# A two-block transformer kernel: the second model's layers start with the first pair's gate tiles

## The reference, cut to what matters

```
mod = silu(c) @ w_ada[l] + b_ada[l];  shift, scale, gate = split(mod, 3)
h = rms_norm(x, norm_g[l]) * (1 + scale) + shift
gq, gk, gv, glr, gz, dq, dk, dv, dz = split_columns(h @ w_in[l])
gq, gk, gv = split(silu(causal_depthwise_conv(concat(gq, gk, gv), conv_w[l])))
log_a = log_sigmoid(glr @ w_gk + b_gk) / 16            # cumulated per chunk of 64 tokens
o_gla  = rms_norm(gated linear attention(gq, gk, gv, log_a), g_out) * silu(gz)
o_diff = rms_norm(differential attention(dq, dk, dv)) * silu(dz)
x = x + gate * (concat(o_gla, o_diff) @ w_out[l])
```

## Time and profile before

| | |
|---|---|
| median of 3 runs | 1962.71 us |
| the profiled execution's own time | 1966.36 us |
| its span, first to last instruction | 1964.6 us |
| TensorE matmuls busy | 1852.8 us (94%) |
| VectorE, ScalarE, GpSimd busy | 1060.0, 877.7, 875.4 us |
| mean granted TensorE clock | 0.978 of full speed |

### The profile page before, as it was taken

The page is one execution under the profiler, slowest core; times in us unless marked ns, Lnnn a source line. Parts: engine busy times, 40 slices in busy tenths (PEclk is TensorE's granted clock), DMA queues, the critical chain, the costliest instruction groups (busy, mean ns, idle before and its releaser), DMA issues.

```text
span 1964.6 us, 26448 instructions
## 1 busy us (share of the span) xinstructions
PE 1852.8 (94%) x8566; PEld 1448.0 (74%) x8566; DVE 1060.0 (54%) x1731; ACT 877.7 (45%) x1385; POOL 875.4 (45%) x1064
## 2 busy tenths in 40 slices
PE   7999989999999999999899999998999988999988
PEld 5666667887888788888788778886776656776756
DVE  5666646612643577787566115523665553674561
ACT  6667643411433455655444214323554533554441
POOL 3323246655665334344147556653543315443323
PEclk9999999999999999999899999998999988999999
DMA  4111125433543222112145334422222112222212
GB/s 151 59 60 53 54 59 167 161 96 107 166 134 96 86 65 65 63 54 66 43 150 171 96 107 153 155 88 75 86 65 65 54 43 86 72 69 65 65 43 75
DMA packets 49660, 176.36 MB, mean 90 GB/s; under 512 B 5649, under 2 KB 5777, under 8 KB 49569
## 3 DMA queue, kind: packets, MB, share of 16 engines
q1 hardware_dynamic: 42368, 148.99, 24.5%
q10 hardware_dynamic: 7200, 26.22, 4.0%
HBM read 173.08 MB, written 2.10 MB: 89 GB/s over the span
## 4 chain that ended last, share of the span: by engine, by line
PE 76%; DVE 10%; ACT 7%; issue 5%; POOL 1%; DMA 0%; DVEq 0%; ACTq 0%; SPq 0%; POOLq 0%
PE ps_g L234 22%; PE ps_g L238 21%; PE ps_g L241 21%; PE ps_zt L939 2%; PE ps_s L1429 1%; PE ps_o L1490 1%; PE ps_o L967 1%; ACT w_hi L206 1%; PE ps_o L495 1%; DVE scr L1603 1%; PE ps_zt L485 1%; PE ps_s L386 1%; DVE scr L1125 1%; PE ps_zt L477 1%; DVE scr L443 1%
## 5 line engine op out<-in xcount | busy, mean ns | idle before, releaser
L214 POOL TENSOR_TENSOR w_lo<-raw,w_hi 128x256 fp32r<-128x256 f32 x936 | 764.6, 847 | 899.5 <-ACT w_hi L206 899.0
L206 ACT ACTIVATE w_hi<-raw 128x1024 fp32r<-128x1024 f32 x274 | 288.9, 1054 | 383.3 <-PE ps_g L241 378.0
L234 PE MATMUL ps_g<-h_hi,w_hi 128*128 128x512 f32 x1424 | 407.0, 414 | 32.7 <-ACT h_hi L295 11.6
L238 PE MATMUL ps_g<-h_lo,w_hi 128*128 128x512 f32 x1424 | 377.7, 394 | 0.9 <-DVE h_lo L267 0.9
L241 PE MATMUL ps_g<-h_hi,w_lo 128*128 128x512 f32 x1424 | 374.9, 392 | 0.3 <-DVE w_lo L222 0.3
L234 PEld LDWEIGHTS ps_g<-h_hi,w_hi 128*128 128x128 f32 x1424 | 259.5, 191 | 119.0 <-issue 54.2
L238 PEld LDWEIGHTS ps_g<-h_lo,w_hi 128*128 128x128 f32 x1424 | 270.6, 190 | 61.6 <-DVE h_lo L267 2.0
L241 PEld LDWEIGHTS ps_g<-h_hi,w_lo 128*128 128x128 f32 x1424 | 270.0, 190 | 58.4 <-DVE w_lo L222 0.7
L234 PE MATMUL ps_g<-a_hi,w_hi 128*128 128x512 f32 x768 | 206.5, 405 | 16.8 <-DVE a_lo L1637 7.5
L238 PE MATMUL ps_g<-a_lo,w_hi 128*128 128x512 f32 x768 | 197.8, 393 | 0.0
L241 PE MATMUL ps_g<-a_hi,w_lo 128*128 128x512 f32 x768 | 197.6, 393 | 0.0
(11 more groups left out here) (167 smaller groups left out, 2027.1 us busy)
## 6 DMA issues: line engine op xcount, KB each, us to landing
raw<-weights SPq DMA_DIRECT2D x274, 512.0 KB, 3.5
scr<-ada_weights ACTq DMA_DIRECT2D x48, 512.0 KB, 4.1
x<-x_tiles SPq DMA_DIRECT2D x8, 256.0 KB, 5.7
y<-x SPq DMA_DIRECT2D x8, 256.0 KB, 3.3
scr<-csil_dram ACTq DMA_DIRECT2D x2, 512.0 KB, 4.9
lvmask<-level_masks SPq DMA_DIRECT2D x1, 512.0 KB, 8.4
mats<-squares SPq DMA_DIRECT2D x1, 448.0 KB, 6.8
vecs<-vectors SPq DMA_DIRECT2D x1, 95.5 KB, 2.0
```

The source lines that it names most:

```text
L206: nc.scalar.activation(w_hi[:, t.rep % 2], raw[:, raw_slot(t)], ACT.Copy).then_inc(whi_ready, 1)
L214: ins = nc.gpsimd.tensor_tensor(w_lo[:, t.rep % 2, ks], raw[:, raw_slot(t), ks], w_hi[:, t.rep % 2, ks].bitcast(F32), ALU.subtract)
L234: nc.tensor.matmul(bank[:], w_hi[:, t.rep % 2, kk], rhs(k)[0], start=(first and n == 0), stop=False)
L238: nc.tensor.matmul(bank[:], w_hi[:, t.rep % 2, kk], rhs(k)[1], start=False, stop=False)
```

## The change

1. The two z tiles of the first GLA pair come first (tiles 0 and 1), then glr (tile 2), then the pair's four convolution tiles (3 to 6); the other tiles keep their places.
2. Tiles 0 and 1 work on x times gain (norms "4" and "6", made with `early_hi` and `early_lo` while the tiles ahead finish, so 8 activations and 8 VectorE operations more per layer). VectorE multiplies their results by the root into `z_b`. What the shift adds, W's, is made by 8 float32 matmuls of one column for each of the two tiles (`shift_pe`), copied by ScalarE.
3. The full h is made as before, into the other pair of buffers (`h_buf` swaps `h_hi`, `h_lo` with `a_hi0`, `a_lo0`), with a copy of tile 0 and tile 1 out of PSUM and two `split_hi` among its steps. Tiles 2 and 3 take it in halves, in turn.
4. The silu of tiles 0 and 1 is spread over later halves: `zlog` (four activations: absolute value, add W's, exp, ln), `zmin`, `zexp`, the product.
5. The decay gate moves from the pair's halves 0 and 1 to its halves 3 and 5, after that half's taps. It has its own buffer.
6. The absolute value of the convolution tiles moves from VectorE to ScalarE, into the `ln` step.

In the diff, the parts are the lists, TensorE's start, ScalarE's start, `zlog` and `ln` on ScalarE, and VectorE's start.

```diff
+        OWN["gla0"] = {i: list(OWN["gla"][i]) for i in OWN["gla"]}
+        for _i, _z in ((5, 0), (9, 1)):
+            OWN["gla0"].setdefault(_i, []).append(("zlog", _z))
+            OWN["gla0"].setdefault(_i + 2, []).append(("zmin", _z))
+            OWN["gla0"].setdefault(_i + 4, []).extend([("zexp", _z), ("evac3", 4 + _z)])
...
                     if it[0] == "gla":
-                        due[0].append(("gate", it[1]))
-                        due[1].insert(0, ("gate2", it[1]))
+                        due[3].append(("gate", it[1]))
+                        due[5].append(("gate2", it[1]))
...
+        def start_pe(pe, l):
+            T, n = T_B2 + l * B2_TILES, 5 + 2 * l
+            first = b2_rhs(n - 1)
+            shift_pe(pe, l, 0)
+            gemm(pe, At(T), T, first, H1, True, False, h_waits(n - 1), (x_ready, (6 + l) * KT - 1))
+            norm_pe(pe, 4 + l)
+            gemm(pe, At(T), T, first, H2, False, True, h_waits(n - 1))
+            shift_pe(pe, l, 1)
+            gemm(pe, At(T + 1), T + 1, first, ALL, True, True, None, (x_ready, (6 + l) * KT))
+            hi, lo = h_buf(n)
+            for half in (H1, H2):
+                for i in (2, 3):
+                    t, slot, bank = At(T + i), (T + i) % 2, ps_g[(T + i) % 2]
+                    pe.wait_ge(whi_ready, t.of(1, 1))
+                    pe.wait_ge(*reader(i - 2, l))
+                    for k, _ in half:
+                        pe.wait_ge(hhi_ready, KT * n + k + 1)
+                        nc.tensor.matmul(bank[:], w_hi[:, slot, k], hi[:, k], start=(k == 0), stop=False)
+                    for k, _ in half:
+                        pe.wait_ge(h_ready, KT * n + k + 1)
+                        nc.tensor.matmul(bank[:], w_hi[:, slot, k], lo[:, k], start=False, stop=False)
+                    if half is H2:
+                        pe.wait_ge(wlo_ready, t.of(1, 1))
+                        for k in range(KT):
+                            ins = nc.tensor.matmul(bank[:], w_lo[:, slot, k], hi[:, k], start=False, stop=(k == KT - 1))
+                        ins.then_inc(tile_used, 1)
...
+                if s[0] == "start":
+                    rstd_act(act, 4 + l)
+                    for k in range(KT):
+                        norm_hi(act, l, k)
+                        if k == 1:
+                            split_hi(act, At(T + R_TILE))
+                        elif k == 3:
+                            act.wait_ge(ws_done, 2 * l + 2)
+                            act.activation(ws_b, ps_o[:, 0:2], ACT.Copy).then_inc(ws_ready, 2)
+                        elif k == 5:
+                            split_hi(act, At(T + R_TILE + 1))
+                    split_hi(act, At(T + R_TILE + 2))
...
+                elif s[0] == "zlog":
+                    act.activation(g_ls.buf, u, ACT.Abs, bias=ws).then_inc(g_ls.abs_ready, 1)
+                    act.wait_ge(g_ls.abs_ready, n.v + 1)
+                    act.activation(u, u, ACT.Identity, bias=ws)
+                    g_ls.act(act, n)
...
+                elif s[0] == "ln" and it[0] == "gla" and s[1] < 4:
+                    act.wait_ge(cv_done, (l * GLA_PAIRS + it[1]) * 12 + 3 * c + 3)
+                    act.wait_ge(b_ls.ready, n.v)
+                    act.activation(b_ls.buf, cv_b[c % 2], ACT.Abs).then_inc(b_ls.abs_ready, 1)
+                    b_ls.act(act, n)
...
+                if s[0] == "start":
+                    for k in range(KT):
+                        if k == 2:
+                            nc.vector.memset(acc[:], 0.0).then_inc(acc_zero, 1)
+                        if k >= 2:
+                            norm_lo(dve, l, k - 2)
+                        norm_tmp(dve, l, k)
+                        if k in (3, 6):
+                            i = k // 4
+                            dve.wait_ge(tile_used, T + i + 1)
+                            nc.vector.tensor_tensor(z_b[i], ps_g[(T + i) % 2][:], rstd_x, ALU.mult).then_inc(z_out, 1)
```

More of the change, by code:

```diff
@@ L1294, in schedule @@
         def schedule():
-            steps = [("gemm", 0, 0), ("gemm", 0, 1), ("gate_in",)]
+            steps = [("start",), ("gate_in",)]
             left = {}
@@ L1298, in schedule @@
             for it in ITEMS + [None]:
[L1299 to L1300 removed]
+                first = it == ITEMS[0]
+                n = 0 if it is None else (8 if first else 12 if it[0] == "gla" else 8)
+                due = [list(left.get(i, [])) for i in range(20)]
                 if it:
[L1302 to L1303 removed]
+                    own = OWN["gla0" if first else it[0]]
+                    for i in own:
+                        due[i] += [s + (it,) for s in own[i]]
                     if it[0] == "gla":
[L1305 to L1306 removed]
+                        due[3].append(("gate", it[1]))
+                        due[5].append(("gate2", it[1]))
                 if before:
@@ L1311, in schedule @@
                 for half in range(n):
-                    steps.append(("gemm", FIRST_TILE[it] + half // 2, half % 2))
+                    if not first or half >= 2:
+                        steps.append(("gemm", FIRST_TILE[it] + half // 2, half % 2))
                     steps += due[half]
-                left = {i - n: due[i] for i in range(n, 16) if due[i]}
+                left = {i - n: due[i] for i in range(n, 20) if due[i]}
                 if it is None:
                     steps.append(("split",))
-                    for i in range(16):
+                    for i in range(20):
                         steps += due[i]
@@ L1327, in build_program @@
         SWISH = [s[1:] for s in STEPS if s[0] == "evac3"]
-        SILUS = [s if s[0] == "gate" else s[1:] for s in STEPS if s[0] == "gate" or s[1:] in SWISH and s[0] == "evac"]
+        SILUS = [s[1:] for s in STEPS if s[1:] in SWISH and s[0] == "evac"]
         def nth(order, key, l):
@@ L1353, in build_program, with log_of @@
         b_ls, b_turn = LogSig("b_ls", bls_b), Turn("b_turn", ps_t)
+        g_ls, LOGS = LogSig("g_ls", res[1][4]), [s for s in STEPS if s[0] in ("gate", "zlog")]
+        z_b, ws_b = [scr2[:, 14], scr2[:, 15]], sml[:, 61:63]
+        ws_done, ws_ready, z_out = ev("ws_done"), ev("ws_ready"), ev("z_out")
+        def log_of(s, l):
+            g_ls.buf = res[1][4] if s[0] == "gate" else scr2[:, 12 + s[1]]
+            return nth(LOGS, s, l)
         b_unit = Unit("b_unit", M_HEADS, DH, bsq_b, brstd_b)
@@ L1407, in b2_pe @@
                 it = s[-1]
-                if s[0] == "gemm":
+                if s[0] == "start":
+                    start_pe(pe, l)
+                elif s[0] == "gemm":
                     tile, half = s[1], s[2]
-                    gemm(pe, At(T + tile), T + tile, h_rhs, H2 if half else H1, not half, bool(half),
-                         h_waits(4 + l) if tile == 0 else None,
-                         reader(tile - 2, l) if tile >= 2 and not half else None)
+                    gemm(pe, At(T + tile), T + tile, b2_rhs(5 + 2 * l), H2 if half else H1, not half, bool(half), None,
+                         None if half else reader(tile - 2, l))
                 elif s[0] == "gate":
@@ L1698, in b2_pool @@
             for s in STEPS:
-                if s[0] == "gemm" and s[2] == 0:
+                if s[0] == "start":
+                    for i in range(2):
+                        pool.wait_ge(ws_done, 2 * l + i + 1)
+                        split_lo(pool, At(T + i + 1))
+                    split_lo(pool, At(T + R_TILE + 1))
+                    split_lo(pool, At(T + R_TILE + 2))
+                elif s[0] == "gemm" and s[2] == 0:
                     split_lo(pool, At(T + s[1] + 1))
@@ L1716, in build_program @@
                 for name in ("ng00", "ng01", "ng10", "ng11")]
+        GAIN += [lambda d, l=l: mod[:, l, bass.ds(d + KT, 1)] if not isinstance(d, int) else mod[:, l, KT + d:KT + d + 1]
+                 for l in range(2)]
         @block.sync
```

154 lines of the change are left out of this document (89 added, 65 removed).

## The result

Slower. The changed kernel takes 1972.12 us (median of 9 runs, 1968.9 to 1977.58); beside it on the same chip the kernel before took 1963.08 (1962.11 to 1965.26, 9 runs): ratio 1.0046, 95% interval 1.0035 to 1.0057, so 9.0 us more. I had forecast 1957.2 (1946 to 1967), faster. The profiled execution of the changed kernel took 1977.38, its span is 1975.4; that is 10.8 over the span before. The nine runs fall into two groups, 1968.9 to 1969.74 at a mean clock of 0.983 or 0.984 and 1975.12 to 1977.58 at 0.979 to 0.982, with the median between them; the profiled execution is one of the upper group.

A forecast was written before the change was run, and what follows sets the result against it. TensorE's matmuls (94% of the span) were taken to bind, then the convolution loop (5.82 a turn for a 5.44 tile). The starts' 11.3 and 11.2 shrink to 2.75 per layer: 2 x 2.75 = 5.5, 1962.7 - 5.5 = 1957.2; range 1946 to 1967.

The forecast's parts named there:

- A: Moment when the start's first four tiles are done and the next begins; forecast 1379.1 and 1684.2, 11.3 and 11.2 earlier.
- three signs of being wrong: Tile 4 not starting before 1385; six turns under 41 or over 48; low clock in over two short stretches, 1410 to 1445.
- the six turns: ScalarE's taps-to-taps times from the second to the eighth taps: 8.7, 6.3, 9.8, 4.9, 9.75, 6.2, sum 45.7.
- 13.2: Length of VectorE's norm chain in the start: 11.75 before, plus the memset (0.3) and two PSUM copies of 0.65 each.
- taps 2 to 3 ... 6.3: First pair's turn in the GLA loop: zlog's four activations (2.96) lie beside VectorE's taps, so 6.3.
- taps 2 to 3: 6.2: Second pair's turn from taps 2 to taps 3 in the GLA loop, the last of six, claimed at 6.2.
- two longer turns: Turns from taps 1 to 2 in both pairs, with the gate ahead of the split: 8.7 and 9.75.
- Those pauses cost nothing more while the clock holds.: TensorE's waits in the GLA stretch, some 1.6 for tile 9 and 3 for tile 10, claimed to add nothing further.
- third rival: Clock falls in new pauses ahead of tile 10; TensorE loses 8.2, the kernel is 7 slower, 1969.8; chance 0.13.
- first rival: VectorE slowed by its neighbour: z's four operations take 1.22 instead of 0.69, 1 to 2 on the chain, 1960.7; chance 0.27.
- second rival: Convolution loop doesn't bind, so the start's 11.2 stay in both layers: 1940.2, chance 0.10; half of it, 1948, 0.08.
- From there to the layer's end nothing is changed.: From the layer's first statistic to its end, no change in time; a shift stays a shift.

The follow-up runs named there:

- x4: Changed kernel with only the first of four pieces of each second-model w_lo made, the rest left out; 1953.29 us, ratio 0.9945 to the kernel before.
- x2: Changed kernel with both pairs' gate2 (minimum and scans) one half later, at half 6; 1972.32 us, ratio 1.0041 to the kernel before.
- x8: Kernel before with only the gate's steps moved to halves 3 and 5, with its own buffer for the logarithm; 1977.99 us, ratio 1.0069.
- x1: Changed kernel with the second pair's gate back at its first two halves; 1966.5 us, ratio 1.0010 to the kernel before.
- x14: x10 with both gates' matmul ahead of the second tile and their activations between the first two taps; 1956.51 us, ratio 0.9961 to the kernel before.
- x15: x14 with the convolution tiles' absolute value back on VectorE; 1955.87 us, ratio 0.9956 to the kernel before.
- x5: Kernel before with only the first of four pieces of each second-model w_lo made, the control for x4; 1957.72 us, ratio 0.9963.
- x13: Kernel before with each convolution tile's exp and logarithm behind the next tile's taps on ScalarE; 1970.81 us, ratio 1.0030.
- x10: x6 with the first pair's gate between its first and second taps, its absolute value on ScalarE; 1959.77 us, ratio 0.9970 to the kernel before.
- x12: x10 with both gates between the first two taps, and each tile's absolute value, exp and logarithm behind the next tile's taps; 1966.14 us, ratio 1.0004.
- x3: Changed kernel with the convolution tiles' absolute value back on VectorE; 1975.89 us, ratio 1.0063 to the kernel before.
- x6: x1 with z's activations cut apart and put ahead of each even half's exp; 1963.29 us, ratio 0.9996 to the kernel before.
- x9: Kernel before with only the convolution tiles' absolute value moved from VectorE to ScalarE; 1972.55 us, ratio 1.0044.

## Why the prediction was wrong

By the marks of the first table, the profiled span is some 16 longer than forecast (10.8 longer than before, not 5.5 shorter). Of this, 5.6 lies in the two starts (2.2 in each from the norm's sum to A, 1.2 ahead of the two sums), 8.0 between A and the statistic, nearly all of it in the turns, and 2.6 behind the second statistic. Of the three signs of being wrong that I had named, one came: the six turns add up to over 48.

**The new start: right in kind, 2 us short.** The first pair's work on x without the root keeps TensorE busy and at 2.4 GHz (1.00 in both windows). The sum came at 1357.36 (1356.9 forecast); the shift matmuls took 1.84 for 16 (1.70 until the next matmul started), where I took 1.0 within bounds of 0 to 2.0. In the second layer, where the first of them stands ahead of the sum, this is the 0.7 by which it is later than forecast. VectorE's first product came 2.51 after the sum, for 2.66; of the 1.0 more before, which I put down to the fallen clock, 0.4 was the memset that stood ahead of the product (1359.21). A came 24.4 after the sum, not 22.2. The term "13.2" of VectorE's norm chain was mis-sized: it ran 16.0 (from 1359.87 to 1375.9). Its timeline shows operations of 1.1 and more for 0.75, and beside them `w_lo`'s four pieces 4.29 for 2.82. ScalarE waits for these operations, so its second split ended 11.2 after the chain's start, not 9.9, and TensorE, for which I had no wait there, stood 1.31 for it.

```profile
1363.85 1.11 DVE L307 SCALAR_TENSOR_TENSOR scr<-x,mod,scr 128x512 f32<-128x512 f32 x1
1364.89 0.68 DVE L1689 TENSOR_TENSOR scr<-ps_g,scr 128x512 f32<-128x512 f32 x1
1365.49 1.32 DVE L302 SCALAR_TENSOR_TENSOR a_lo<-scr,mod,a_hi 128x512 fp32r<-128x512 f32 x1
...
1369.32 0.75 DVE L302 SCALAR_TENSOR_TENSOR a_lo<-scr,mod,a_hi 128x512 fp32r<-128x512 f32 x1
```
```profile
1357.02 2.82 POOL L215 TENSOR_TENSOR w_lo<-raw,w_hi 128x256 fp32r<-128x256 f32 x4 [5.49 <-ACT w_hi L207]
1363.12 4.29 POOL L215 TENSOR_TENSOR w_lo<-raw,w_hi 128x256 fp32r<-128x256 f32 x4 [3.28 <-ACT w_hi L207]
```

x4 takes three of four pieces away, the chain runs 14.0 and A comes after 22.49: those 1.9 are shown to be the split's. Before, the chain ran with no split beside it (the last piece ended at 1358.90, the chain began at 1359.61), and I had put two there without a price. The Trainium skill, "GPSIMD Engine Reference", Specifications, says that VectorE's instructions with two SBUF inputs collide with GpSimd on their shared interface; the rows agree (the copy at 1364.89, which reads PSUM, took its 0.68).

**The failing step: "taps 2 to 3 ... 6.3", and "taps 2 to 3: 6.2".** They took 8.64 and 7.79, which is 3.9 of the 4.1 by which the six turns exceed my 45.7; the others were close (8.52, 10.63, 4.91, 9.32 for 8.7, 9.8, 4.9, 9.75). The step failed twice. I followed ScalarE's queue and asked of VectorE only when the minimum comes: I left out that the taps themselves wait for the silu product of two tiles earlier, and that gate2 puts nine instructions ahead of it on VectorE. And with those nine in the sum, at the 1.57 that the scans take in the earlier trace rows, the turn would still have come out near 6.5: beside the split the scans took 3.71. The taps' wait for the product is 2.10, and the scans are 2.14 longer. Neither half does it alone. With gate2 moved away (x2) the first pair's turn is 6.45. With most of the split cut but gate2 in place (x4) the two turns are 7.09 and 6.52. So the order puts VectorE's queue into ScalarE's turn, and in the first pair nearly all of the wait is VectorE slowed beside GpSimd's split.

**The gate's place.** I priced its two longer turns and still let the start's gain cover them. With the split as it is, it doesn't: the place alone costs 13.5 in the old order (x8), and in the changed kernel one gate put back gives 7 (x1). With both gates where ScalarE idles and z's activations in its gaps the kernel is 7.7 (x14) and 8.6 (x15) faster than before by the ratios. Of the 20.5 by which the changed kernel's two starts are shorter, x14 has 12.4 left at its two statistics.

**"Those pauses cost nothing more while the clock holds."** It did not hold. TensorE stands 2.87 ahead of tile 9, whose bank the late taps 0 set free (the row at 1418.37; forecast 1.6), and 0.63 for `w_hi` ahead of tile 10 (forecast 3). The windows at tile 9 show the low level, 1.2 GHz. The last two rows are the second layer's, one at the same pause of 2.87 and one ahead of the statistic:

```profile
1416.40:1418.30 1.90, 0.00 (x0) 0.00 (x0) 1.83 (x4) 0.98 (x3) 1.41 (x3) 0.96 0.00 0
1418.40:1420.00 1.60, 1.60 (x4) 1.31 (x5) 1.60 (x3) 1.54 (x3) 1.60 (x2) 0.50 0.00 0
1420.00:1423.20 3.20, 3.20 (x14) 2.55 (x14) 3.13 (x5) 1.36 (x3) 0.59 (x1) 0.76 0.33 106
1423.20:1428.00 4.80, 4.17 (x19) 3.09 (x19) 1.97 (x5) 3.54 (x6) 1.29 (x2) 1.00 0.11 42
...
1725.20:1732.20 7.00, 5.37 (x13) 4.14 (x14) 6.89 (x10) 3.64 (x7) 3.69 (x4) 0.51 0.25 70
1756.00:1759.60 3.60, 3.60 (x12) 2.82 (x11) 2.09 (x3) 2.09 (x4) 0.16 (x1) 0.53 0.43 148
```

So the third rival's mechanism came, one tile earlier than it said. In the first layer it was far cheaper than its 8.2: 1.6 at the low level and about half of the next 3.2, so 3.1 us in which TensorE lost 1.6. In the second layer it was dearer. The clock's shortfall in the last two rows (0.49 of 7.00 and 0.47 of 3.60) is 5.1, some of it while TensorE was waiting anyway, and the way from A to the statistic is 1.4 longer there than in the first layer. The rival's time (1969.8) was near, but the clock is the smaller part of the way to it.

The first rival, VectorE slowed by its neighbour, was right in kind and closer to the cause than my forecast was. It named the four operations of z and priced them at 1 to 2; the dear ones were the scans (3.71 for 1.57) and the start's. The second rival, that the loop doesn't bind, fell (x5, x13).

**"From there to the layer's end nothing is changed."** It takes 2.2 and 2.6 longer. The first of these is the next start: there the norm's sum stands behind the shift matmuls and half a gemm, and comes 6.4 after the last eight out matmuls begin (1659.58 to 1665.96), for 4.3 before (1656.32 to 1660.58). So 2.1 of the 2.2 are explained, of which I had 1.4. The 2.6 of the second layer come with a lower clock. Here are 208 us and then 20 us from the second statistic on, of the changed kernel and, behind the dots, of the kernel before:

```profile
1760.50:1968.50 208.00, 189.11 (x822) 136.81 (x821) 98.01 (x246) 87.54 (x163) 67.62 (x93) 0.94 0.19 59
1760.50:1780.50 20.00, 16.14 (x62) 11.73 (x61) 9.23 (x13) 10.50 (x17) 6.58 (x9) 0.91 0.12 32
...
1752.30:1960.30 208.00, 187.18 (x834) 135.95 (x833) 98.00 (x246) 87.46 (x163) 67.60 (x93) 0.97 0.20 61
1752.30:1772.30 20.00, 16.20 (x71) 11.94 (x70) 9.88 (x14) 11.57 (x19) 6.59 (x9) 1.00 0.15 41
```

All kernels with the whole split part by that clock of the first 20 us. Where it is 1.00 (before, x1, x2, x10, x12, x15) the way from the second statistic to the end takes 212.2 to 212.5, and where it is 0.91 (changed, x3, x6, x8, x9, x13, x14) 214.2 to 214.9. TensorE's pause in these 20 us is the same, 2.15 before and 2.17 changed, 14.6 behind the statistic. So these 2 us go with the clock, and not with the turns. The stretch behind the first statistic parts alike in the kernels with the new start, 213.4 to 214.0 against 215.4 to 216.0, but for x15 (213.3 at 0.91). Why a like pause is followed by the low level in one execution and not in another stays open (each kernel has one profiled execution), and with it the changed kernel's spread, which goes with the mean clock.

## What to carry to other kernels

In a loop over two engines, write down for each instruction of the turn what it waits for, its output buffer's last reader too, and then everything that stands ahead of that reader on its own engine: a step moved into a gap of one queue can stand ahead of the reader in the other. In this kernel the time won at a stage's start was kept only as far as the loop behind it wasn't longer than a tile; so price each part of a change by itself, and against the kernel before, since one part can cost more than the whole. And where a chain on VectorE reads two SBUF operands, look at what GpSimd does beside it before taking its durations over: here the split cost the new order some 12 us more than the old, and the whole loss is 9.

## What the runs showed that I had not expected

- Eight scans of 128x64 took 1.57 alone and 3.71 beside GpSimd's split (x2: 4.58), more than twice: while a piece of `w_lo` ran, a scan took some 0.77, about the 0.71 of the piece itself, and otherwise 0.26. Operations of 128x512 went from 0.75 to between 1.1 and 1.3.
- A step's worth depended on its neighbours: the absolute value on ScalarE is 8.6 slower in the kernel before (x9, most of it not explained by the trace), 3.3 faster in the changed one (x3, at the edge of what can be told), and makes no difference that can be told between x14 and x15.
- A pause of 2.87 on TensorE was followed by a low clock within the next rows, and one of 2.15 in some executions and not in others, while the 1.0 of the new start held through the wait of 1.31 that stands in it.
